# Two layers beside one gather stream: context's chain split, its state and half of the second pair's parked in DRAM

## What is computed

```
hc, hl = modulate(rmsnorm(ctx)), modulate(rmsnorm(x))       # adaLN, rows from w_ada
q, k, v, mlqk, mlv, mlo, gates, bg, cg, xv, gate = h @ w_in
da  = differential attention: latents look at context and latents, context at context
ml  = mLSTM, forward and backward over chunks of 128; latents start from context's end states
cv  = bg * conv3(cg * xv)
x  += g1 * ((sig(gate_da)*(da@w_da) + sig(gate_ml)*(ml@w_ml) + sig(gate_cv)*(cv@w_cv)) @ w_o)
h2  = modulate(rmsnorm(x)); q = h2 @ wq                     # PEER
per token, 8 heads: the 16 best of 128 x 128 experts by product keys (top 16, top 16, top 16 of 256)
x  += g2 * sum_k gate_k * gelu(u[e_k] . h2) * v[e_k]        # 128 rows of u and of v for each token
```

## Time and profile before

| | us |
|---|---|
| median of 3 runs | 5952.52 (5951.0 to 5960.44) |
| profiled run | 5959.65 |
| its span, first to last instruction | 5957.4 |

### The profile page before, as it was taken

One profiled execution on the slowest core, in us unless ns is written; L12 is line 12 of the kernel. 1 busy time (PEld: TensorE's weight loads), 2 busy tenths in 40 slices (PEclk: granted clock), 3 DMA queues, 4 the chain that ended last, 5 costly groups with the idle time before them and its releaser, 6 DMA issues.

```text
span 5957.4 us, 64624 instructions
## 1 busy us (share of the span) xinstructions
PE 3649.6 (61%) x22248; PEld 2524.4 (42%) x22248; DVE 2907.9 (49%) x6855; ACT 1675.0 (28%) x4743; POOL 1390.3 (23%) x1297
## 2 busy tenths in 40 slices
PE   3889457788775675437455556778435786433333
PEld 1677444566654453224133234667313565311111
DVE  0321747644447544764444444321765443864444
ACT  0200127332432342233322222200224253222222
POOL 0000013212221232223334331000233232133333
PEclk7779779858887787667567667769657798755555
DMA  6434358748896898779999995114688898689998
GB/s 255 153 129 161 118 205 312 282 182 303 323 373 234 304 408 359 272 270 394 375 398 410 405 405 233 46 54 153 253 328 342 311 375 342 229 339 406 409 410 361
DMA packets 326553, 1730.30 MB, mean 290 GB/s; under 512 B 95984, under 2 KB 108624, under 8 KB 138832
## 3 DMA queue, kind: packets, MB, share of 16 engines
q0 software_dynamic: 184320, 1342.26, 57.0%
q1 hardware_dynamic: 134224, 362.92, 16.8%
q10 hardware_dynamic: 7680, 20.98, 1.3%
HBM read 1706.68 MB, written 19.23 MB: 290 GB/s over the span
## 4 chain that ended last, share of the span: by engine, by line
PE 39%; DMA 28%; DVE 15%; ACT 6%; issue 4%; DVEq 4%; POOL 2%; ACTq 2%; SPq 1%; PEldq 0%; POOLq 0%; PEld 0%
PE psum L467 27%; DMA arena<-in_uv,arena 23%; PE psum L815 5%; DVE arena L2096 4%; POOL arena L1156 2%; DVE arena L2003 1%; DVE arena L1996 1%; DMA arena<-in_w_ada 1%; DVE arena L1997 1%; PE psum L427 1%; PE psum L648 1%; PE psum L649 1%; DMA arena<-in_w_mix 1%; ACT arena L1515 1%; DMA arena<-in_norm_g 1%
## 5 line engine op out<-in xcount | busy, mean ns | idle before, releaser
L1156 POOL DMA_INDIRECT arena<-in_uv,arena x1280 | 1386.0, 1083 | 4533.0 <-PE psum L815 3019.0
L2096 DVE CUSTOM_DVE_ANT_0 arena<-arena 128x1024 f32<-128x1024 f32 x1280 | 1556.5, 1229 | 1341.7 <-DMA arena<-in_uv,arena 1284.3
L467 PE MATMUL psum<-arena 128*128 128x256 f32 (+2 forms) x8480 | 2024.7, 399 | 213.0 <-DVEq L1535 91.3
L815 PE MATMUL psum<-arena 128*32 128x256 f32 x10240 | 990.3, 524 | 1539.3 <-ACTq L1516 1525.7
L467 PEld LDWEIGHTS psum<-arena 128*128 128x128 f32 (+1 forms) x8480 | 1672.2, 201 | 591.9 <-issue 114.3
L815 PEld LDWEIGHTS psum<-arena 128*32 128x32 f32 x10240 | 334.8, 137 | 2106.7 <-ACTq L1516 1733.4
L1508 ACT ACTIVATE arena<-arena 128x2 f32<-128x2 f32 x640 | 131.0, 205 | 1795.1 <-DVEq L2098 1671.3
L1515 ACT ACTIVATE arena<-arena 128x32 f32<-128x32 f32 x1280 | 341.9, 314 | 45.6 <-issue 1.4
L427 PE MATMUL psum<-arena 128*128 128x128 f32 (+1 forms) x680 | 135.1, 357 | 342.4 <-DVE arena L1594 119.1
L1512 ACT ACTIVATE arena<-arena 128x1 f32<-128x1 f32 x1280 | 307.5, 287 | 46.6 <-issue 2.7
L427 PEld LDWEIGHTS psum<-arena 128*128 128x128 f32 (+1 forms) x680 | 102.7, 185 | 386.3 <-issue 165.7
(11 more groups left out here) (211 smaller groups left out, 2752.4 us busy)
## 6 DMA issues: line engine op xcount, KB each, us to landing
arena<-in_w_in SPq DMA_DIRECT2D x92, 1024.0 KB, 7.0
arena<-in_w_mix SPq DMA_DIRECT2D x120, 768.0 KB, 8.2
arena<-in_w_ada SPq DMA_DIRECT2D x32, 1536.0 KB, 16.4
arena<-in_w_wq SPq DMA_DIRECT2D x40, 1152.0 KB, 5.5
arena<-in_w_wo SPq DMA_DIRECT2D x20, 1024.0 KB, 9.0
arena<-in_uv,arena POOLq DMA_INDIRECT x1280, 12.4
arena<-h_rows ACTq DMA_DIRECT2D x160, 128.0 KB, 7.2
arena<-ada_rows SPq DMA_DIRECT2D x15, 512.0 KB, 7.7
```

The lines of the kernel that those rows point to most:

```text
L467: ins = mm(out, a, b, start=(i == 0), stop=(i == last))
L815: ins = mm(acc_bank(u)[32 * q:32 * q + 32, gg * 256:gg * 256 + 256], DIAG[:, c, :], RING[:, sl, D + q * 256:D + (q + 1) * 256], start=(h, ...
L1156: pool.indirect_dma_start(RING[:, sl, :], None, io["uv"], bass.IndirectOffsetOnAxis(PICKED_U[b][:, h_, tg, a:a + 1], 0)).then_inc(gathered ...
L2096: V_.tensor_tensor_reduce(out=RING[:, sl, 0:D], in0=RING[:, sl, 0:D], in1=XT[:, gg, :], scale=1.0, scalar=0.0, op0=ALU.mult, op1=ALU.add, ...
```

## The change

Layer 0 now runs as layer 1 does. Segment a holds context's `norm1`, `kv`, `mlp` and `ml` alone; then `park` stores context's normed tiles and mLSTM output (1.57 MB) to DRAM; then come pair 1's `norm1`, `qkv`, `mlp`, `mc`, pair 2's `norm1`, `kv`, `mlp`, `edge`, and `da` of pair 1, `ml_back`, `mln` and `merge` of pair 1. The stream begins with pair 1's units. Beside it stand: pair 1's routing; a `swap` that stores pair 2's state (3.87 MB) and then loads context's back (1.57 MB); context's `q`, `da`, `mc`, `mln`, `merge` and routing; a `swap` that loads pair 2's state (3.87 MB); pair 2's rest and routing; then layer 1's first stages as before. In `park` and `swap` PE, ACT and DVE wait for the semaphore `swapped`, and SP stays in the stage till its DMAs have landed. A routing step now costs 24 in `steps` (before: 12, and 28 in the one routing named in `OVERLAPPED`), so more groups go beside it. There are 302 weight chunks, before 277. The pieces of `ada1` go with context's `norm1`, `mlp` and `ml` and with pair 1's `norm1`.

```diff
-UNITS = [(0, t, f) for t in range(NT) for f in range(2)] + [(1, t, f) for t in range(CT, NT) for f in range(2)]
+UNITS = [(0, t, f) for t in (2, 3, 0, 1, 4, 5) for f in range(2)] + [(1, t, f) for t in range(CT, NT) for f in range(2)]
...
-        return [(28.0 if (l, pairs) in OVERLAPPED else 12.0)] * PH
+        return [24.0] * PH
...
-    a = [(k, 0, (0,)) for k in ("norm1", "qkv", "da", "mlp", "ml", "mc", "mln", "merge", "route")]
-    b = [(k, 0, both) for k in ("norm1", "qkv", "da", "mlp", "ml", "mc", "mln")] + [("merge", 0, (1,)), ("route", 0, (1,))]
-    c1 = [("merge", 0, (2,)), ("route", 0, (2,))] + [(k, 1, (0,)) for k in ("norm1", "kv", "mlp", "ml")]
...
+    def first_pair(l):
+        return [(k, l, (2,)) for k in ("norm1", "kv", "mlp", "edge")] + [("da", l, (1,)), ("ml_back", l, both), ("mln", l, (1,)), ("merge", l, (1,))]
+    def second_pair(l):
+        return [("q", l, (2,)), ("da", l, (2,)), ("ml_on", l, both)] + [(k, l, (2,)) for k in ("mc", "mln", "merge", "route")]
...
+    a = [(k, 0, (0,)) for k in ("norm1", "kv", "mlp", "ml", "park")] + [(k, 0, (1,)) for k in ("norm1", "qkv", "mlp", "mc")] + first_pair(0)
+    b = [("route", 0, (1,))] + [(k, 0, (0,)) for k in ("swap", "q", "da", "mc", "mln", "merge", "route")]
+    c = [("swap", 0, (2,))] + second_pair(0)
+    c2 = [(k, 1, (0,)) for k in ("norm1", "kv", "mlp", "ml")] + ahead
+    e1 = [("route", 1, (1,))] + second_pair(1)
...
+                for dst, src in out:
+                    sp.dma_start(dst, src).then_inc(s("swapped"), 16)
+                if out and back:
+                    sp.wait_ge(s("swapped"), cnt["swapped"] + 16 * len(out))
+                for src, dst in back:
+                    sp.dma_start(dst, src).then_inc(s("swapped"), 16)
+                sp.wait_ge(s("swapped"), nxt("swapped", SWAPS[kind, pairs]))
```

140 lines of the change are left out of this document (77 added, 63 removed).

## The result

The changed kernel takes 6144.98 us (median of 4 runs, 6143.41 to 6148.11) against 5956.48 for the kernel before (4 runs beside it, 5951.0 to 5967.84): ratio 1.0316, 95% interval 1.0304 to 1.0329, so 3.2% slower. The forecast was 6088, with a range of 5995 to 6155: 135 us more than before, where 188 were measured. The profiled execution has a span of 6141.9 us.

The account below looks back on a forecast made before the run. Stretches without gathers were taken as one engine's chain, gather-full ones as DMA-bound, routings as neither. Terms 989+2813+507.3+1163.5+620 gave a span of 6093 us; plus 2, less 7, the forecast was 6088, range 5995 to 6155.

Parts of the forecast that it names:

- The part ahead of the stream: Stages before the first gather's group, priced from windows without gathers: 989 us, bounds 970 to 1005, before 732.6.
- The routings: Five routings beside gathers, priced by groups a step, each beyond the fifth at 5.0 us: 345, 318, 348, 335, 308 us.
- The swaps: Two waits for DRAM moves in layer 0: 30 us for the first, 18 for the second (bounds 10 to 30).
- The chains: Stages between routings beside gathers: context's 458 us, pair 2's 584, layer 1's pair 2 520.5 with its groups kept.
- Layer 1's first stages: Stages beside 112 groups, 55 fewer than before, with DMA setting the time at 98% share: 712 us, before 1003.6.
- The last stretch: The kernel's end, with 16 groups fewer at 5.2 us each: 620 us, before 703.3.
- That the stream runs full: Rival: stages from the first gather on reach 366 GB/s, not 340, and take 2620 us; kernel 5895 us, chance 10%.
- Cheap swaps and routings at their low bounds: Rival: swaps cost only their bytes (13.6 and 9.7 us), routings 36 us less; kernel 6027 us, chance 20%.
- Starving six-group steps: Rival: each group beyond four costs 5.0 us, prefetch is lost, routings add 48 us, crowded merges at 6.2; 6145 us, 12%.
- Blocking swaps: Rival: SP can't issue weights in a swap and stores go slowly, over 100 us in the first; 6175 us, 6%.
- That the change does nothing: Rival: the new order gives back ahead of the end exactly what it adds ahead of the stream; 5953 us, 4%.
- Why so little comes back: Gains of 98 us beside gathers and 23 at the end against 256 added, put down to added dense work and dear routing groups.

Follow-up runs that it names:

- e1: The changed kernel with park and both swaps done twice in a row, the second stores going to a spare tensor: 6170.57 us, ratio 1.035.
- e7: The changed kernel with layer 0's gathers moved from beside the dense stages into two blocks of their own: 6820.14 us, one run.
- e9: The kernel before with step cost 24 in pair 2's layer 0 routing, 10 in the last, and layer 0's stream as one sequence: 5923.88 us, ratio 0.9949.
- e12: e9 with a head's scores done ahead of the next head's queries in routing steps: 5837.8 us, ratio 0.9799.
- e5: The changed kernel with eight stream positions ahead of each of the first two final norms: 6127.72 us, ratio 1.0286.
- e2: The changed kernel with old routing step costs (12; 28 in the two routings that feed themselves): 6200.89 us, ratio 1.0412.

## Why the prediction was right, point by point

**The bound and the method.** Cutting the span at barriers and pricing each new stage by its twin in the trace of before gave 6093 for a span of 6141.9, 0.8% off. Of the change itself the forecast had the way and for the most part the mechanism, but the size was short: 135 us of 188. The measured time lies in the stated range, above the 6050 to 6125 that the forecast gave its own sum. All terms but the routings erred low or were right. The 49 us of span are 14.0 in the last stretch, 10.3 in layer 1's first stages, 10.2 in the second swap, 5.8 and 3.5 in the chains of layer 0, 11.7 in that of layer 1, 3.8 in the first swap and 1.9 ahead of the stream, less 12.0 in the five routings.

The part ahead of the stream came out at 990.9 for 989: the block with a twin took 508.8 for 507.3. Inside it two terms were low. Context's `mlp`, with a piece of `ada1` in it, took 69.0 for 56.5: PE waited 10.2 us in it for a weight chunk, with four 1.5 MB loads of `w_ada` issued in the same 69 us, so their loads were not all hidden. `park` took 14.7 for 10: SP issued its stores 9.4 us into it, and they landed 3.9 and 4.8 us later. Lower than their rows were pair 1's `mlp` and `mc` (45.9 and 59.4 for 49.0 and 63.5), context's `kv` with pair 1's `norm1` (45.7 for 49.3) and `ml` (74.1 for 77.6). That the sum was right to 2 us is luck: the errors met.

**The routings** came out at 346.6, 313.8, 345.6, 335.6 and 300.4 for 345, 318, 348, 335 and 308, the best part of the forecast. They were right without the cause: the steps of four and five groups from which I priced already held the 8 us that DVE waits for scores, which I had not seen, and which the run with the scores first took away. The forecast's own numbers leave room for it: 17 us of top 16 and four groups at 2.5 are 27, and the four-group step took 35.6. (The forecast also calls both steps steps of four; only the one at 2562.18 is, the one at 2597.73 has five, as its next words say.)

**The swaps.** 33.8 for 30, 28.2 for 18. The second is the term mis-sized most in proportion. Its DMAs took what I gave them (the 2758 KB one landed after 17.7 us), but SP issued them only 8.5 us into the stage, behind the hand-over of the routing's last picks, as SP's row shows (the first swap's stores stood behind the same 8.5 us):

```profile
2155.06 0.82 SPq L1132 DMA_DIRECT2D arena<-parked  x2
```

The forecast had counted the bytes and not what stands ahead of them on SP's queue.

The Trainium skill, in "DMA: Bandwidth & Descriptors", section "Anatomy of one DMA — SWDGE (gpsimd) path", gives by its formula, which it fits to DMAs issued from GpSimd, 8.5 us for the 2758 KB store, an estimate. The store, issued by SP, landed after 17.1 us among gathers and 10.1 without them (e1, e7), so the rows are near it where the engines were free and at twice its figure where they were not.

**The chains** came out at 461.5, 589.8 and 532.2 for 458, 584 and 520.5. The first sum is right in part by luck: `q` took 21.1 for 31 (17.9 bare, e7), `da` 62.8 for 55 and the merge 265.7 for 261. In the second `q`, `da` and `ml_on` took 183.6 for 171, `mc` and `mln` 121.2 for 126. For the merges the forecast names 5.0 a group as the least, but its own figures give (392.0 - 250.3 - 35) / 23 = 4.6; the 5.0 taken was right. In the last chain the forecast kept every position, but one had moved from `q` to `mc` (3 and 12 for 4 and 11). `mc` took 88.0 us for 79.4, `da` 93.7 for 88.0 (its first part, up to the turns, 81.3 for 72.2), `q` 31.4 for 34.7. The old order's runs with `q` at 3 and `mc` at 12 show the same: e9 has 86.1, 93.6 and 30.6, e12 85.3, 93.5 and 30.5. So it isn't the order but the moved position. `mc` holds 25 gathers for 22 and stands at a DMA share of 0.98, which goes with its 9 us; why `da` is longer behind a shorter `q` stays open.

**Layer 1's first stages** took 722.3 for 712: they ran at 0.95 of the DMA, not at the 0.98 of the earlier trace rows. The two `norm1` stages in them, 38.4 and 42.5 us at a DMA share of 0.67 and 0.73, are not full, and with 112 groups in place of 167 they are a larger part of the stretch; `ml` ran at 0.94 and the last `mc` at 0.92, the other four stages at 1.01 to 1.02.

**The last stretch** took 634.0 for 620, some 11 of the 14 by the final norm without cover, as e5 showed. The old order has eight positions ahead of each of the first two final norms and the new one none; the forecast left this unpriced.

**From the span to the median** I took 5 us off; it is 3 more. The profiled execution of before lay 7 us above its median, that of the changed kernel 1 below, which no row could tell.

**The rivals.** That the stream runs full (5895) fell: 344 GB/s over the 2842 us, as the forecast's 340 had it, and not 366. Cheap swaps and routings at their low bounds (6027) fell with the rows above. Starving six-group steps (6145) gave the measured time to the us, by luck: a sixth group cost 5.0 and no prefetch was lost, and no routing came out over 2 us above its forecast. Blocking swaps (6175) fell with the first swap's 33.8 us, the stores at 17.1 and 9.2, and with e1. That the change does nothing (5953) fell with the measured time itself. Two signs were wrong: layer 1's first stages weren't at 98% DMA, and POOL issued no gather between 1342 and 1372.6 us, in the first swap, as it waited for PE, which stood and freed no slot. Of the signs of being wrong none came: six-group steps took 41.1 us and not under 38, no stretch between the routings passed 380 GB/s but single stages, and segment a ended at 990.9.

**Why so little comes back** was put down to new dense work and to dear groups in routings. The bare runs bear out the first (143 of 189 us). The second wasn't it: a sixth group did cost 5.0 us, but taking groups out of the routings (e2) lost 56 us more, and the rest is 54 us of overlap that 115 us of dense work took along when they left.

## What to carry to other kernels

Work moved out from beside a full stream gains nothing there (54 us less of PE's work in c2 were worth 4 us), so before an order is changed for the stream's sake, run the dense work and the stream apart and see how much of each is hidden; here 258 us were added ahead of it and only about 115 left its side. Where engines walk one list with fixed lags, look in every step at what stands between the arrival of one engine's data and the work that another waits for: the scores behind the next head's queries cost 125 us, four times what the best order or density of the study gave. And a cost table that seems to give a constant price may hide a step, as the third group did.
